# A three-group output projection: groups of 416, 416 and 256 tokens, the last with tokens on partitions

## What is computed

```
merged = sigmoid(ga + b_gate[:D]) * y_a + sigmoid(gg + b_gate[D:]) * y_g      # 1088 x 2048
o      = merged @ w_out                                                        # 2048 x 2048 weights
h      = h + o * rsqrt(mean(o * o, axis=-1) + eps) * norm_post                 # mean over a token's 2048 features
```

## Time and profile before

| | us |
|---|---|
| median of three runs | 2829.95 |
| the profiled execution | 2828.88 |
| its span, first to last instruction | 2827.1 |
| TensorE busy | 2736.5 (97%) |
| VectorE busy | 2125.1 (75%) |
| ScalarE busy | 1209.3 (43%) |
| GpSimd busy | 80.0 (3%) |

### The profile page before, as it was taken

One profiled execution on the slowest core, in us unless ns is written; L12 is line 12 of the kernel. 1 busy time (PEld: TensorE's weight loads), 2 busy tenths in 40 slices (PEclk: granted clock), 3 DMA queues, 4 the chain that ended last, 5 costly groups with the idle time before them and its releaser, 6 DMA issues. The chain is left out here.

```text
span 2827.1 us, 52027 instructions
## 1 busy us (share of the span) xinstructions
PE 2736.5 (97%) x20860; PEld 2595.6 (92%) x20860; DVE 2125.1 (75%) x3375; ACT 1209.3 (43%) x1972; POOL 80.0 (3%) x55
## 2 busy tenths in 40 slices
PE   7999999998999999999999999999899989999996
PEld 7999999998999999999777887877799989999996
DVE  7999778778787877877777777777676877655556
ACT  5344333445354333344556566565522322342331
POOL 0221000000000000000000000000000000000001
PEclk9999999999999999999999999999999999999998
DMA  4455433435344343344656666565634456555564
GB/s 153 165 187 186 143 122 121 135 124 200 102 143 135 121 135 123 121 133 131 193 168 179 184 181 180 163 195 159 213 138 177 171 209 233 165 173 182 188 193 140
DMA packets 234187, 456.95 MB, mean 162 GB/s; under 512 B 23905, under 2 KB 139745, under 8 KB 233073
## 3 DMA queue, kind: packets, MB, share of 16 engines
q1 hardware_dynamic: 233968, 453.91, 49.8%
HBM read 365.90 MB, written 88.47 MB: 161 GB/s over the span
## 5 line engine op out<-in xcount | busy, mean ns | idle before, releaser
L2217 PE MATMUL bank<-th,w_hi 128*128 128x272 f32 x2360 | 686.0, 291 | 3.2 <-DVE w_lo L1458 2.2
L2217 PE MATMUL bank<-tl,w_hi 128*128 128x272 f32 x2360 | 681.9, 289 | 0.0
L2217 PE MATMUL bank<-th,w_lo 128*128 128x272 f32 x2360 | 681.3, 289 | 0.0
L1445 DVE TENSOR_TENSOR w_lo<-w_raw,w_hi 128x1024 fp32r<-128x1024 f32 x224 | 273.8, 1222 | 235.0 <-ACT w_hi L1011 234.6
L2217 PEld LDWEIGHTS bank<-th,w_hi 128*128 128x128 f32 x2360 | 444.4, 188 | 6.3 <-issue 3.1
L2217 PEld LDWEIGHTS bank<-tl,w_hi 128*128 128x128 f32 x2360 | 444.5, 188 | 1.0 <-issue 1.0
L2217 PEld LDWEIGHTS bank<-th,w_lo 128*128 128x128 f32 x2360 | 444.1, 188 | 0.0
L1026 ACT ACTIVATE w_hi<-w_more 128x1024 fp32r<-128x1024 f32 x236 | 250.2, 1060 | 424.6 <-PE bank L2217 222.0
L1011 ACT ACTIVATE w_hi<-w_raw 128x1024 fp32r<-128x1024 f32 x224 | 236.8, 1057 | 367.5 <-PE bank L2531 239.1
L1458 DVE TENSOR_TENSOR w_lo<-w_more,w_hi 128x1024 fp32r<-128x1024 f32 x236 | 297.6, 1261 | 93.0 <-ACT w_hi L1026 92.8
L2195 PE MATMUL bank<-uh,w_hi 128*128 128x272 f32 x1024 | 316.0, 309 | 13.3 <-DVE w_lo L1445 8.5
(11 more groups left out here) (287 smaller groups left out, 5644.4 us busy)
## 6 DMA issues: line engine op xcount, KB each, us to landing
w_raw<-in_w_tiles SPq DMA_DIRECT2D x344, 512.0 KB, 4.1
w_more<-in_w_tiles SPq DMA_DIRECT2D x120, 512.0 KB, 3.6
p_scratch<-stage SPq DMA_DIRECT2D x44, 544.0 KB, 3.0
gl<-p_scratch SPq DMA_DIRECT2D x24, 512.0 KB, 5.6
w_pair<-in_w_tiles SPq DMA_DIRECT2D x9, 1024.0 KB, 8.7
gate_scratch<-stage SPq DMA_DIRECT2D x16, 544.0 KB, 3.0
gate_scratch<-stage SPq DMA_DIRECT2D x64, 136.0 KB, 4.2
gate_even<-gate_scratch SPq DMA_DIRECT2D x8, 1088.0 KB, 6.2
```

Of the source, the lines that this page charges most:

```text
L1445: dve.tensor_tensor(w_lo[:, h], w_raw[:, h], w_hi[:, h].bitcast(f32), ALU.subtract).then_inc(s_wlo, 1)
L2217: ins = pe.matmul(out[:, 0:GAW], wt[:, k], ut[:, k], start=start and k == 0 and i == 0, stop=stop and k == HK - 1 and i == 2, skip_group_c ...
```

## The change

- `GRP` becomes 416, 416 and 256 tokens. Groups 0 and 1 are made as before, with wider tiles; `RING_W` keeps two shared buffers at their old size. Buffers are laid out anew; pieces 20 to 22 of the operand all go through one buffer (`Z_ALONE`), not through two in turn.
- The last group has the roles of the operands turned. The 256 tokens are two blocks of 128, stationary; the weights are moving, two feature tiles (256 columns) at a time. A unit `u` is a pair of feature tiles and one half of the depth: 16 units, each with 24 matmuls for each of the two token blocks. Output pairs alternate between banks 2, 3 and 0, 1. Each unit's 1 MB of weights stands in one of two sets of buffers (`last_w`), the old one and a second.
- The output of a pair is [128 tokens, 256 features]. ScalarE squares it with a sum along the free axis as a by-product (`accum_out`), and copies it to `o_tok`. VectorE adds up the parts of the sum. So the sum of squares of a token is a number on its own partition.
- After the last unit, VectorE makes the mean, GpSimd the root, VectorE the diagonal of the roots, for each block of 128 tokens alone. TensorE then multiplies `o_tok` (a block of 128 tokens x 128 features, stationary, full fp32) with the diagonal (moving): the result is the block turned back to features on partitions and scaled by the roots in one. VectorE reads it from PSUM, multiplies it by the norm's weight and adds the residual in one instruction, 32 of them on 128 x 128, and nine stores bring it out.
- `finish` of group 1 now lies beside the 16 units. The 16 scalings and 16 additions behind the last matmul, the spreading, and GpSimd's part in the additions are gone.

The core of the diff (the buffers' layout left out):

```diff
-GRP = [(0, 364), (364, 362), (726, 362)]
-GW = 364
+GRP = [(0, 416), (416, 416), (832, 256)]
+GW = 416
+RING_W = 364
+LAST_T = GRP[2][1] // P
+LAST_UNITS = 2 * (D_MODEL // P // 2)
...
# SP
+            def load_unit(u):
+                i, kh = divmod(u, 2)
+                if u == 0:
+                    sp.wait_ge(s_mo, 2 * KT)
+                for r in range(2):
+                    if u > 0:
+                        sp.wait_ge(s_wlo, 2 * (PASS_LAST + u - 2) + r + 1)
+                    sp.dma_start(last_w[u % 2][0][:, r], w_src(ROW_OUT + 2 * i + r, kh)).then_inc(s_w[r] if u % 2 else s_wb, 16)
...
+            for u in range(LAST_UNITS):
+                if u + 2 < LAST_UNITS:
+                    load_unit(u + 2)
+                if u > 0:
+                    store_y(1, KT + u - 1, u - 1, (u - 1) % 2)
+                if u + 1 < KT:
+                    load_x(1, KT + u + 1, u + 1, (u + 1) % 2)
+                if u in (3, 6, 9, 12):
+                    ...
+                    sp.dma_start(x_last[:, k:k + 4], x_view[:, k:k + 4, a:a + w]).then_inc(s_xl, 16)
...
+            for t, k, n in stores:
+                sp.wait_ge(s_add, KT * t + k + n)
+                sp.dma_start(y_view[:, k:k + n, a + t * P:a + t * P + P], x_last[:, k:k + n, t * P:t * P + P]).then_inc(s_yl, 16)
# ScalarE
+            def hi_unit(u):
+                raw, hi, _ = last_w[u % 2]
+                for r in range(2):
+                    ...
+                    act.activation(hi[:, r], raw[:, r], ACT.Copy).then_inc(s_whi, 1)
+            def take_pair(i):
+                for t in range(LAST_T):
+                    src = bank[last_bank(i, t)][:, 0:2 * P]
+                    act.wait_ge(s_mo, 2 * (2 * KT + 2 * i + 1) + t + 1)
+                    act.wait_ge(s_oev2, 2 * KT + max(0, 2 * LAST_T * i + 2 * t - 1))
+                    act.activation(square, src, ACT.Square, scale=D_MODEL ** -0.5, accum_out=parts[:, i, t:t + 1]).then_inc(s_oev2, 1)
+                    act.activation(o_tok[:, t, 2 * P * i:2 * P * i + 2 * P], src, ACT.Copy).then_inc(s_oev2, 1)
+            for u in range(LAST_UNITS):
+                if u + 1 < LAST_UNITS:
+                    hi_unit(u + 1)
+                if u > 0 and u % 2 == 0:
+                    take_pair(u // 2 - 1)
+            take_pair(KT // 2 - 1)
# VectorE, in the loop over units
+                if u + 1 < LAST_UNITS:
+                    lo_unit(u + 1)
+                if u == 0:
+                    roots(3, GRP[1][1], bank[6])
+                if u == 1:
+                    spread(3, GRP[1][1], bank[6:7], rso)
+                    dve.wait_ge(s_rstd, 6)
+                    finish(1, 0, KT, 0)
+                if u > 0:
+                    finish(1, u, KT + u, u % 2)
# VectorE, behind it
+            mean_last(0)
+            diagonal_last(0)
+            dve.wait_ge(s_xl, 16 * KT // 4)
+            for t in range(LAST_T):
+                for b, ks in turned(t):
+                    dve.wait_ge(s_tr, KT * t + ks[-1] + 1)
+                    for k in ks:
+                        x = x_last[:, k, t * P:t * P + P]
+                        dve.scalar_tensor_tensor(out=x, in0=bank[b][:, (k - ks[0]) * P:(k - ks[0]) * P + P], scalar=norm_sb[:, 1, k:k + 1],
+                                                 in1=x, op0=ALU.mult, op1=ALU.add).then_inc(s_add, 1)
+                        if (t, k) == (0, 1):
+                            mean_last(1)
+                        if (t, k) == (0, 5):
+                            diagonal_last(1)
# TensorE
+            def last_products(u, t):
+                i, kh = divmod(u, 2)
+                out = bank[last_bank(i, t)][:, 0:2 * P].rearrange("p (r c) -> p r c", r=2)
+                _, hi, lo = last_w[u % 2]
+                rows_of_t = slice(t * P, t * P + P)
+                for k in range(HK):
+                    for j, (ut, wt) in enumerate(((mh[2], hi), (mh[2], lo), (ml[2], hi))):
+                        ins = pe.matmul(out, ut[kh * HK + k][:, rows_of_t], wt[:, :, k], ...)
+                ins.then_inc(s_mo, 1)
...
+            for t in range(LAST_T):
+                pe.wait_ge(s_oev2, 2 * KT + 2 * LAST_T * (KT // 2 - 1) + 2 * t + 2)
+                pe.wait_ge(s_dg, 4 + t + 1)
+                for b, ks in turned(t):
+                    if (t, b) == (1, 4):
+                        pe.wait_ge(s_add, 2)
+                    for k in ks:
+                        pe.matmul(bank[b][:, (k - ks[0]) * P:(k - ks[0]) * P + P], o_tok[:, t, k * P:k * P + P], diag[:, t], start=True,
+                                  stop=True).then_inc(s_tr, 1)
+TURN_BANKS = (((4, 2), (5, 2), (6, 4), (7, 4), (2, 4)), ((3, 4), (0, 4), (1, 4), (4, 4)))
```

More of the change, by code:

```diff
@@ L966, in _ @@
             load_x(0, 0, 0, 0)
[L967 to L986, removed]
-                    sp.wait_ge(s_mo, 2 * KT)
[L988 to L992, removed]
@@ new lines, in pair @@
+            def pair(i):
+                for r in range(2):
+                    m = 2 * i + r
+                    if isinstance(m, int) and m == KT - 1:
+                        load_x(1, KT, 0, 1 - r)
+                    else:
+                        load_x(0, m + 1, m + 1, 1 - r)
+                    next_w(PASS_OUT + KT + m, m)
+                    store_y(0, m, m, r)
+            pair(0)
+            load_unit(0)
+            with sp.Fori(1, KT // 2 - 1) as i:
+                pair(i)
@@ L1382, in _, with pair @@
                 tile(0, m, m % 2)
[L1383 to L1390, removed]
-                pair(KT // 2 - 1)
+            def pair(i):
+                for r in range(2):
+                    tile(1, 2 * i + r, r)
+            pair(0)
+            with act.Fori(1, KT // 2 - 1) as i:
+                pair(i)
+            pair(KT // 2 - 1)
+            for u in range(LAST_UNITS):
[4 more added lines that the diff above has]
+            take_pair(KT // 2 - 1)
         @block.gpsimd
@@ L1430, in _ @@
                 gla_roots(it, DEC if it == N_IT - 1 else P)
-            for n in range(3):
-                roots(n + 2, 3)
-            w = GRP[2][1]
-            for k in range(1, KT, 2):
-                pool.wait_ge(s_sc2, k + 1)
-                if k == 1:
-                    pool.wait_ge(s_xl, 16 * KT // 4)
-                pool.tensor_tensor(out_sb[2][:, k, 0:w], out_sb[2][:, k, 0:w], x_last[:, k, 0:w], ALU.add).then_inc(s_add[1], 1)
+            for n in range(2):
+                roots(n + 2, 4)
+            for t in range(LAST_T):
+                pool.wait_ge(s_rst, 2 * 4 + t + 1)
+                pool.tensor_tensor(root[:, t:t + 1], mean[:, t:t + 1], minus_half[:], ALU.pow).then_inc(s_rsp, 1)
         @block.vector
@@ L2140, in tile @@
                     behind = g > 0 and isinstance(m, int) and m == 0
+                    last = isinstance(n, int) and n == 2 * KT - 1
                     if behind:
@@ L2152, in tile @@
                         lo_merged(*merged_pieces(m))
[L2153 removed]
+                    if not last:
                         lo_w(PASS_OUT + n + 1, 1)
@@ L2535, in _ @@
             pe.wait_ge(s_bq, 6 * (N_BR - 1) + 2)
-            for g in range(3):
+            for g in range(2):
                 def pair(i):
```

156 lines of the change are left out of this document (108 added, 48 removed).

## The result

The changed kernel takes 2813.5 us (median of 4 runs, 2811.5 to 2815.5), the kernel before 2830.1 in the same comparison (2828.0 to 2830.6): ratio 0.9943, 95% interval 0.9926 to 0.9960. It is faster by 16.6 us by the medians and by 16.1 us by the ratio; 2813 was forecast. In the comparisons further down, one execution of a variant (5781 us, the norm's row in four loads) and three of the kernel before (2888.9, 3765 and 11174 us) were far slower than the rest and are left out. The profiled execution took 2815.5 us, with a span of 2813.3, so it lies 2.0 us above its median.

What follows compares the result with a forecast made beforehand. TensorE's matmuls were taken to bound the three groups, ahead of a 28.0 us tail. -1.5 + 0.65 + 0.9 leaves the last product at 2799.1; a 10.9 us tail gives span 2810.0, execution 2811.8, median 2813 us; range 2808 to 2820.

Steps and rivals of the forecast that it cites:

- The bound and the place of the gain: Last stage: three groups are paid by their matmuls; the change can gain in the 28.0 us tail and lose ahead of it.
- Part 1: Matmul streams of the three groups: 416 columns at 189.4 ns, 256 at 119.4; +16.6, +17.8, -35.9, together -1.5 us.
- Part 2: First tile of group 0: wider early pieces delay the start of its second half pass, +0.65 us (0 to 1.5).
- Part 3: Sums and roots of groups 0 and 1: two more fp32 instructions in each of two steps, 0.11 us each, +0.9 us.
- Part 4: Feeding the last group's 5.73 us units: vector work and weight loads fit, costed at nothing, up to +3 us for single waits.
- Part 5: Tail behind the last product: turning 7.5 us, VectorE 0.95, last store 2.4; 10.9 us against 28.0, -17.1 us.
- The half clock in the turning: Rival, in the tail: the granted clock halves during the turning products, +4.5 us, 2817.5; chance 0.14.
- The floor: Rival, last group: 256-column products cost as 272 or a little more, +5.3 us, 2818; chance 0.18 together with single load waits.
- The loads as a bound: Rival, 16 units: ScalarE's copies wait for weight DMA; with 11.5 us landing +28 us, 2841; chance 0.06.

## Why the prediction was right, step by step

- **The bound and the place of the gain.** Right: the stream ahead of the tail took as long as before, the tail lost 15.7 us (17.1 forecast).
- **Part 1.** Right. 118.3 ns at 256 columns (119.4 taken, 119.2 to 119.6), 188.9 in group 1 and 190.0 in group 0 at 416 (189.4; 188.7 to 190.1). By stretch +16.2, +18.4, -34.7, where parts 1 and 3 together give +16.6, +18.2, -35.4. No floor. Tokens as the stationary operand and the two runs of 128 columns, which got no price, cost at most a little: the old form with the same width and the second set of buffers is at 116.2 ns on average (half passes from 113.3 to 118.9), 2 ns less, which is 1.5 us over the group.
- **Part 2.** +0.7 us for +0.65. The half clock behind this wait went in the changed kernel (the wait is 1.8 us, the next two products are 0.27 us apart, then 0.19), as the range allowed. In the kernel before it cost 1.3 us, so the +16.2 us of group 0 is +17.6 for the width and -1.3 for the clock; that it comes so near the forecast 16.6 is in part luck. That it went was luck too: in the run with the cut and two sets of buffers it came behind the same wait of 1.78 us.
- **Part 3.** +1.5 us for +0.9. From the first instruction of the sums to the next product it is 0.80 us (0.55 before), for the spreading 1.09 (0.59), in each of the two groups: 0.19 us for each added instruction, not the 0.11 that the row of six gives.
- **Part 4.** The result was right, with one wait of 0.7 us for its "nothing", which the text did not find: it looked at SP's order inside the loop, not at the load of the second unit behind the last store. Two margins were tested: 1.2 us more on VectorE is carried, 0.5 MB more in each unit as well. But a load to landing was taken from the earlier trace rows as 4.1 us, and in the busy stretch it is 5.8 us (up to 7.6). The 8.0 us of cover held, with less to spare than the text says. The range's 3 us for waits was enough.
- **What the text did not see.** It never asked what the second set of buffers was worth, since it never worked out the narrow tile with one. By its own numbers (4.1 + 1.06 + 1.23 us against 5.7) the cut without it loses, and the run shows it, by 21 us. The same slip made both expectations for that run miss.
- **Part 5.** The tail was 1.4 us longer than the 10.9 forecast. The mis-sized term is VectorE's step, 0.21 us for 128 elements taken from a product of tensors in SBUF: with a PSUM source and a scalar it is 0.26 from start to start. It becomes the bound, 32 x 0.26 = 8.3 us, as the text's own upper bound (0.28, +1.0 us) has it. By the Trainium skill, VectorE: DVE Perf Modes, section "The TRN2 errata", an instruction that reads PSUM costs 120 cycles and one for each element at 0.96 GHz, 258 ns at 128 elements, where one from SBUF has 58 in place of 120, 194 ns. The trace agrees for PSUM (0.26 from start to start, while one instruction lasts 0.34) and nearly for SBUF (0.21). The other part is the last store, 3.0 us for 2.5: when it is issued, at 2810.37 us, four stores in front of it are still under way (the last of them lands at 2812.52, it lands at 2812.92). The turning was right: 7.3 us for 7.5. That the root lies hidden was right, and is shown: bare it costs 1.8 us.
- **The rivals.** The half clock in the turning did not come, not even behind a gap of 1.9 us. By the Trainium skill, TensorE: Matmul & The Clock Gate, Part 4, it would have been the case only if the gate saw these products like transposes; 7.3 us of them alone ran at 1.00. The floor did not come. The loads as a bound came only when they were made so: 1 MB more in each unit gave the waits at the landing time that the rival names, 8 us and more, and there a cycle of two units took 14 to 15 us, near the rival's sum (3.5 us and a landing of up to 10.2).
- **The number is nearer than its terms.** The span of 2813.3 us is 3.3 over the 2810.0 that the sum gave: 1.4 in the tail, 0.7 in the wait, 1.2 ahead of the change. But the profiled execution lies 2.0 us above its median where the one of before lay 1.1 below, so the median hit. That the number hits to 1 us is luck: the pace of group 0 alone, which the sum does not know, moves the time by 4.8 us.

## What to carry to other kernels

A group of fewer tokens is a shorter time to feed for the same weights: before narrowing a tile, add load, copy and subtraction for one buffer, and compare the sum with the tile's new length. Here the second set of buffers decided whether the cut gained or lost. Where a tail is shortened, write down the next bound for each engine and for the stores with the price of exactly that operand form; here three lay side by side (turning 7.3 us, VectorE 8.3 us, stores 2.1 MB at 290 GB/s, that is 7.2 us, from 1.8 us on), so taking one away brought almost nothing.

## What the runs showed of the hardware

**One program, two paces.** In group 0 the products of 416 columns start 190.0 ns apart through the whole group in 8 of 11 profiles with this width, and 183.3 ns apart from the second or third half pass on in the other 3, at clock 1.00 in both. The first and last of 34 in the changed kernel's profile, then in its repetition's (same program):

```profile
2439.66 0.35 PE L2638 MATMUL bank<-mh,w_hi 128*128 128x416 f32 x1
...
2445.92 0.35 PE L2638 MATMUL bank<-mh,w_hi 128*128 128x416 f32 x1
```

```profile
2439.80 0.35 PE L2638 MATMUL bank<-mh,w_lo 128*128 128x416 f32 x1
...
2445.85 0.35 PE L2638 MATMUL bank<-mh,w_lo 128*128 128x416 f32 x1
```

6.26 us against 6.05 us for 33 steps; over the group it is 4.8 us. Group 1 was at 188.9 each time, with the same instructions. All eleven profiles start group 0 at 190 ns. In the three, the pace changes where the stream has paused, behind the wait in front of the 25th product twice and at the change to the second tile once, and holds from there on. What decides it is open; no run was made for it. It cannot explain the spread of the changed kernel's runs (2808.8 to 2815.0) by itself: the repetition's profile has the faster pace and still took 2813.7 us, its median, because its group 0 started 3.1 us later (2415.0 for 2411.9), behind longer waits in the branch stage (2.36 us for 0.96 at one place). It was not in the range as such, and 4.8 us is half of what the change gains by the turned form.

**Products with the diagonal** of 128 x 128 in full fp32 start 0.114 us apart (7.3 us for 64), at full clock, with nothing else on TensorE.

**A wait of 2 us may or may not bring the half clock.** In front of the 25th product of group 0 TensorE waits 1.78 us both in the changed kernel and in the run with the cut and two sets of buffers. The same stretch behind it, in the former, then in the latter:

```profile
2419.00:2422.00 3.00, 3.00 (x18) 2.96 (x17) 2.93 (x7) 0.00 (x0) 0.00 (x0) 1.00 0.36 127
```

```profile
2419.00:2422.00 3.00, 3.00 (x11) 2.84 (x10) 2.93 (x7) 0.00 (x0) 0.00 (x0) 0.50 0.39 145
```

At half the clock the products start 0.347 us apart, and the group is 1.4 us longer for it. In the kernel before, behind 2.24 us, the clock fell too. Behind the 1.93 us with both roots made late it did not. With the megabyte more in each unit it fell behind waits of 2.35 and 2.86 us (the windows with 0.90 and 0.51 above), and not behind those of 0.8 us. Just ahead of group 0 it fell behind 1.98 us in that run and stayed behind 2.02 us in the repetition and 2.14 us in the run with both roots late. What decides between the two at about 2 us no run shows.
